# First-layer expert pieces as one 512-wide product into two banks, with the halves added on ScalarE and VectorE

## The reference

```python
def one_chunk(xc):
    ...
    sc, ci = lax.top_k(cand, PEER_TOPK)
    e = jnp.take_along_axis(i1, ci // PEER_TOPK, axis=-1) * PEER_NKEYS \
        + jnp.take_along_axis(i2, ci % PEER_TOPK, axis=-1)
    g = jax.nn.softmax(sc, axis=-1)
    u_sel = u[e]
    v_sel = v[e]
    pre = jnp.einsum("td,thkd->thk", xc, u_sel).astype(f32)
    act = (jax.nn.gelu(pre, approximate=False) * g).astype(v.dtype)
    return jnp.einsum("thk,thkd->td", act, v_sel)
```

## Time and profile before

| | |
|---|---|
| Median of 3 runs | 3540.41 us (3538.41 to 3542.09) |
| Profiled execution: its own time | 3537.68 us |
| Profiled execution: span, first to last instruction | 3535.9 us |
| TensorE matmuls busy | 3373.6 us (95%) |
| TensorE weight loads busy | 2988.4 us (85%) |
| VectorE busy | 2445.0 us (69%) |
| ScalarE busy | 1535.7 us (43%) |
| Mean granted TensorE clock | 0.982 of full |
| TensorE's share of the chain that ended last | 79% |

### The profile page before, as it was taken

The page is one execution under the profiler, slowest core; times in us unless marked ns, Lnnn a source line. Parts: engine busy times, 40 slices in busy tenths (PEclk is TensorE's granted clock), DMA queues, the critical chain, the costliest instruction groups (busy, mean ns, idle before and its releaser), DMA issues.

```text
span 3535.9 us, 54258 instructions
## 1 busy us (share of the span) xinstructions
PE 3373.6 (95%) x20894; PEld 2988.4 (85%) x20894; DVE 2445.0 (69%) x4176; ACT 1535.7 (43%) x1752; POOL 229.4 (6%) x48
## 2 busy tenths in 40 slices
PE   6899999999999999999999999999999999899998
PEld 1889999888888889899998878888878788888787
DVE  6667997777886759995557767556557575555474
ACT  1544454343333534453333335454455454544553
POOL 0005700000000028200000000000000000000000
PEclk9999999999999999999999999999999999999999
DMA  8434467778885234566666765533435455333353
GB/s 360 179 108 158 162 223 253 264 273 281 288 284 180 107 137 177 190 226 229 210 212 234 243 226 203 202 144 120 157 143 191 174 184 198 136 139 145 144 189 133
DMA packets 165987, 689.96 MB, mean 195 GB/s; under 512 B 11701, under 2 KB 78029, under 8 KB 92249
## 3 DMA queue, kind: packets, MB, share of 16 engines
q1 hardware_dynamic: 161432, 663.84, 52.1%
q10 hardware_dynamic: 4290, 22.54, 1.8%
HBM read 650.66 MB, written 35.68 MB: 194 GB/s over the span
## 4 chain that ended last, share of the span: by engine, by line
PE 79%; DVE 12%; ACT 3%; issue 2%; DVEq 1%; DMA 1%; PEld 1%; ACTq 0%; PEldq 0%
PE ps L1074 20%; PE ps L769 16%; PE ps L804 9%; PE ps L775 8%; PE ps L832 8%; PE ps L810 5%; PE ps L1052 3%; PE ps L839 3%; PE ps L860 2%; ACT weights_upper L1321 1%; DVE weights_lower L1744 1%; DMA work<-in_mem 1%; DVE position_hot L2073 1%; PE ps L866 1%; DVE position_hot L2076 1%
## 5 line engine op out<-in xcount | busy, mean ns | idle before, releaser
L1321 ACT ACTIVATE weights_upper<-weights 128x2048 fp32r<-128x2048 f32 x520 | 996.0, 1917 | 1603.2 <-PE ps L769 567.6
L1744 DVE TENSOR_TENSOR weights_lower<-weights,weights_upper 128x2048 fp32r<-128x2048 f32 x476 | 1089.8, 2290 | 643.9 <-ACT weights_upper L1321 643.6
L769 PE MATMUL ps<-hT_lower,weights_upper 128*128 128x256 f32 x2560 | 367.3, 286 | 2.8 <-DVE hT_lower L1757 2.6
L769 PE MATMUL ps<-hT_upper,weights_upper 128*128 128x256 f32 x2560 | 364.1, 285 | 0.0
L769 PEld LDWEIGHTS ps<-hT_lower,weights_upper 128*128 128x128 f32 x2560 | 334.2, 193 | 8.9 <-DVE hT_lower L1757 3.7
L775 PE MATMUL ps<-hT_upper,weights_lower 128*128 128x256 f32 x2560 | 333.6, 283 | 4.1 <-POOL weights_lower L697 4.1
L769 PEld LDWEIGHTS ps<-hT_upper,weights_upper 128*128 128x128 f32 x2560 | 334.7, 194 | 0.0
L775 PEld LDWEIGHTS ps<-hT_upper,weights_lower 128*128 128x128 f32 x2560 | 318.7, 192 | 4.9 <-POOL weights_lower L697 4.9
L804 PE MATMUL ps<-hT_span,weights_upper 128*128 128x512 f32 x1344 | 320.6, 391 | 0.0
L697 POOL TENSOR_TENSOR weights_lower<-weights,weights_upper 128x2048 fp32r<-128x2048 f32 x44 | 229.2, 5223 | 1202.8 <-ACT weights_upper L1321 1202.8
L804 PEld LDWEIGHTS ps<-hT_span,weights_upper 128*128 128x128 f32 x1344 | 247.0, 188 | 47.8
(11 more groups left out here) (375 smaller groups left out, 4202.3 us busy)
## 6 DMA issues: line engine op xcount, KB each, us to landing
weights<-in_parts SPq DMA_DIRECT2D x264, 1024.0 KB, 4.8
weights<-in_experts SPq DMA_DIRECT2D x256, 1024.0 KB, 4.9
scr<-gates SPq DMA_DIRECT2D x32, 1024.0 KB, 8.5
weights<-in_ada_w SPq DMA_DIRECT2D x12, 2048.0 KB, 13.1
work<-in_ada_s SPq DMA_DIRECT2D x96, 256.0 KB, 5.3
gates<-h SPq DMA_DIRECT2D x16, 1024.0 KB, 4.8
gates<-work SPq DMA_DIRECT2D x16, 1024.0 KB, 4.8
mod<-in_row ACTq DMA_DIRECT2D x3, 1536.0 KB, 6.3
```

The costliest lines, as they stand in the source:

```text
L769: m = mm(bank[:, e * T:(e + 1) * T], up[:, c, e * P:(e + 1) * P], s_[:, c, :], start=(e == 0 and n == 0 and c == 0), stop=False, skip_grou ...
L1321: f(upper[:, p_.r % SPLIT, :], raw[:, p_.r, :], ACT.Copy).then_inc(upper_ready, 1)
L1744: v.tensor_tensor(lower[:, s, :], raw[:, p_.r, :], upper[:, s, :].bitcast(F32), ALU.subtract)\
```

## The change

In the interleaved stretch of both layers (first-layer pieces with t at least `AHEAD`, 24 in each layer) `doubled` replaces `by_feature`: one matmul, 512 wide, multiplies a block of upper weights with the lower and the upper part of the input at once. The two parts of the result stand side by side in a bank, so a piece fills two banks, one for each block of 128 experts, and the two halves of each must be added. ScalarE copies the first halves into `gact`, VectorE adds the second halves to them (`halves_added`) and frees the banks, and ScalarE applies Gelu in place one step later (`gelu_of_sum`). The banks are laid out anew: U in 0 and 2, the second banks in 1 (`Ux0`) and 3 (`Ux1`), G in 6 and 7 ahead of acc, the row in 3 in turn with `Ux1`.

```diff
@@ -152,11 +152,17 @@
...
     p.fill("eT", 2, bank=4)
+    p.fill("G", 2, bank=6, times=GROUPS)
     p.fill("acc", 4, bank=4)
-    p.fill("U", 2, bank=0, times=TURNS, parts=1)
-    p.fill("G", 2, bank=2, times=GROUPS)
-    if not before:
-        p.fill("row", 1, bank=2, times=ADA_TILES)
+    p.fill("U", 1, bank=0, times=TURNS, parts=1)
+    p.fill("U", 1, bank=1, times=TURNS, parts=1, start=1)
+    p.fill("Ux0", 1, bank=1, times=TURNS - AHEAD, parts=1)
+    for n, (layer, t, u) in enumerate(expert_order()):
+        if layer == 0 and u == 1 and t >= AHEAD:
+            p.fill("Ux1", 1, bank=3 - t, parts=1, start=t)
+        for tile in range(0 if before else ADA_TILES):
+            if ada_sub_step(KC * tile + KC - 1) + 2 == n:
+                p.fill("row", 1, bank=3 - tile, start=tile)
...
@@ -507,8 +513,11 @@
...
-        hT_up = parts_at("hT_upper", [P, KC, T], hT_at)
-        hT1 = hT_up, parts_at("hT1_lower", [P, KC, T], mod_at)
+        step = (hT_at - mod_at) // (4 * T)
+        hT1_span = parts_at("hT1_span", [P, step + KC, T], mod_at)
+        hT_up = hT1_span[:, step:step + KC, :]
+        hT1 = hT_up, hT1_span[:, 0:KC, :]
+        hT1_both = [hT1_span[:, c:c + step + 1:step, :] for c in range(KC)]
...
@@ -780,6 +789,23 @@
...
+            def doubled(p_, banks, src, both):
+
+
+                up, lo = halves_of(p_, KC)
+                pe.wait_ge(*p_.upper())
+                for e in range(2):
+                    for c in range(KC):
+                        m = mm(banks[e].rearrange("p (n t) -> p n t", n=2), up[:, c, e * P:(e + 1) * P], both[c],
+                               start=(c == 0), stop=False, skip_group_check=True)
+                m.then_inc(upper_used, 1)
+                pe.wait_ge(*p_.lower())
+                for e in range(2):
+                    for c in range(KC):
+                        m = mm(banks[e][:, T:2 * T], lo[:, c, e * P:(e + 1) * P], src[0][:, c, :],
+                               start=False, stop=(c == KC - 1), skip_group_check=True)
+                m.then_inc(parts_done, 1)
...
@@ -1020,16 +1046,21 @@
                 def first_layer(n, t, u):
 
                     pe.wait_ge(*k.free("U", u, t))
-                    by_feature(expert_part(l, 0, n), k.bank("U", u), hT1)
+                    if t < AHEAD:
+                        by_feature(expert_part(l, 0, n), k.bank("U", u), hT1)
+                    else:
+                        second = ("Ux1", t) if u else ("Ux0", 0, t - AHEAD)
+                        pe.wait_ge(*k.free(*second))
+                        doubled(expert_part(l, 0, n), (k.bank("U", u), k.bank(*second[:2])), hT1, hT1_both)
...
                     for tile in range(ADA_TILES if l + 1 < DEPTH else 0):
                         if ada_sub_step(KC * tile + KC - 1) + 2 == n:
-                            pe.wait_ge(*k.free("row", 0, tile))
+                            pe.wait_ge(*k.free("row", tile))
                             pe.wait_ge(S("ada_used"), KC * tile + KC)
-                            mm(k.bank("row")[0:1, :], ones[:, 0:1], ada_acc[tile % 2], start=True, stop=True,
-                               skip_group_check=True).then_inc(k.fill_sem("row"), 1)
+                            mm(k.bank("row", tile)[0:1, :], ones[:, 0:1], ada_acc[tile % 2], start=True, stop=True,
+                               skip_group_check=True).then_inc(k.fill_sem("row", tile), 1)
...
@@ -1459,7 +1490,20 @@
                     act.wait_ge(*expert_part(l, 0, n).done())
                     if t >= AHEAD:
                         act.wait_ge(S("gated"), l * (2 * TURNS) + (2 * (t - AHEAD) + 2))
-                    f(gact[t % AHEAD][:, u, :, :], k.bank("U", u), ACT.Gelu).then_inc(k.empty_sem("U", u), 1)
+                    mine = gact[t % AHEAD][:, u, :, :]
+                    if t < AHEAD:
+                        f(mine, k.bank("U", u), ACT.Gelu).then_inc(k.empty_sem("U", u), 1)
+                        return
+                    banks = k.bank("U", u), k.bank(*(("Ux1", t) if u else ("Ux0", 0)))
+                    for e in range(2):
+                        m = f(mine[:, e, :], banks[e][:, 0:T], ACT.Copy)
+                    m.then_inc(S("hidden_first"), 1)
+
+                def gelu_of_sum(t, u):
+
+                    act.wait_ge(S("hidden_sum"), l * 2 * (TURNS - AHEAD) + 2 * (t - AHEAD) + u + 1)
+                    mine = gact[t % AHEAD][:, u, :, :]
+                    f(mine, mine, ACT.Gelu).then_inc(S("gelu"), 1)
...
                 def ada_take(tile):
 
-                    act.wait_ge(*k.filled("row", 0, tile))
...
@@ -1498,6 +1542,8 @@
...
+                    if n > 2 * AHEAD and expert_order()[n - 1][0] == 0:
+                        gelu_of_sum(*expert_order()[n - 1][1:])
                     if layer == 0:
                         gelu(n, t, u)
...
@@ -2102,7 +2148,10 @@
...
-                    v.wait_ge(*k.emptied("U", u, t))
+                    if t < AHEAD:
+                        v.wait_ge(*k.emptied("U", u, t))
+                    else:
+                        v.wait_ge(S("gelu"), l * 2 * (TURNS - AHEAD) + 2 * (t - AHEAD) + u + 1)
...
@@ -2130,6 +2179,17 @@
...
+                def halves_added(t, u):
+
+                    v.wait_ge(S("hidden_first"), l * 2 * (TURNS - AHEAD) + 2 * (t - AHEAD) + u + 1)
+                    mine = gact[t % AHEAD][:, u, :, :]
+                    second = ("Ux1", t) if u else ("Ux0", 0)
+                    v.tensor_tensor(mine[:, 0, :], k.bank("U", u)[:, T:2 * T], mine[:, 0, :], ALU.add)\
+                        .then_inc(k.empty_sem("U", u), 1)
+                    v.tensor_tensor(mine[:, 1, :], k.bank(*second)[:, T:2 * T], mine[:, 1, :], ALU.add)\
+                        .then_inc(k.empty_sem(*second), 1)
+                    v.drain().then_inc(S("hidden_sum"), 1)
...
@@ -2144,6 +2204,8 @@
                         lower_part(expert_part(l, 0, n + SPLIT))
                     elif l + 1 < DEPTH:
                         lower_part(part(firsts[l + 1], 0, "xbc", n + SPLIT - EXPERTS))
+                    if layer == 0 and t >= AHEAD:
+                        halves_added(t, u)
```

9 lines of the change are left out of this document (5 added, 4 removed).

## The result

| | before | after |
|---|---|---|
| Median of 13 runs each | 3540.99 us (3538.41 to 3549.91) | 3548.66 us (3543.99 to 3550.93) |
| Profiled execution: its own time | 3537.68 us | 3548.97 us |
| Span | 3535.9 us | 3547.2 us |
| Mean granted TensorE clock | 0.982 | 0.975 |

A forecast was written before the change was run, and what follows sets the result against it. TensorE was taken to bound the interleaved stretches. Wide products saving 9.2 us against new waits of 6.6 and 2.7 gave +0.1 us, so a median of 3540.5 us, range 3533.5 to 3547.0.

The forecast's parts named there:

- The gain: First-layer pieces of both interleaved stretches: a wide matmul replaces two, saving 0.19 us a piece, 9.2 us over 48.
- the slack of VectorE and ScalarE: Interleaved stretches: added copies and additions hide behind TensorE's 5.57 us piece; VectorE's fullest layer 0 step keeps 0.9 us.
- the five places: Layer 0: row products of tiles 2 and 5, and later bank 3 uses at tiles 1, 4 and 7, forecast to wait.
- New wait 1: Layer 0, tiles 2 and 5: row products wait for bank 3, just filled by the preceding piece; 3.3 us each, 6.6 total.
- New wait 2: Layer 0, tiles 1, 4, 7: pieces wait for bank 3 until ScalarE takes the row; 0.9 us each, 2.7 total.
- rival B: TensorE's clock falls to half after the two long row-product waits in layer 0: +4.4 us, 3544.9 us; chance 14%.
- The sum: Whole kernel: -9.2 + 6.6 + 2.7 = +0.1 us, so a median of 3540.5 us.
- Theory 2: Formed after the result: the new layout or wide products cost something by themselves, outside the interleaved stretch too.
- A: Layer 0: waits on bank 3 mostly absent; 3533.9 us, or 3531.2 without any new wait; chance 12%.
- C: Interleaved stretches: the wide product saves nothing because its halves are read 40 KB apart; +9.3 us, 3549.8 us; chance 6%.
- D: Layer 0: VectorE falls behind, each of 24 steps 0.4 us late; +9.6 us, 3550.1 us; chance 6%.

The follow-up runs named there:

- Layer 1 alone: The change switched off in layer 0 and kept in layer 1, against the kernel before: 3538.14 us, ratio 0.9990.
- The shift by six products: Six products of zeros added behind piece 87 of layer 0 in the kernel before, nothing else changed: 3551.11 us, ratio 1.0031 against that kernel.

## Why the prediction was wrong

- **The gain** was right: 0.19 us a piece. Layer 1 alone and layer 1 of the changed kernel show 4.8 us by the landmarks, for 4.6 forecast, and the slack of VectorE and ScalarE held. Neither engine made TensorE's matmuls wait outside the five places.
- **New wait 1** was right in place, number and chain: 3.1 us of idle time, a start 3.2 late by the page's own times, for 3.3 forecast. The run with the additions first shows that the subtraction ahead of them was 1.1 us of it, and that ScalarE's copies come next in the chain. **New wait 2** was right: 0.9 us, three times.
- **The step that failed** is the one on the clock. I put the clock behind the two new waits at nothing, since the idle stretches of 3.2 us are "shorter than the one that left the clock alone", and gave 14% to rival B. Two rows of one trace, 3.52 us without and 4.34 us with a fall, are no bound between them. The clock fell behind both waits of 3.13 us, for 4.2 us; the same 3.52 us were followed by a fall in other executions, and in the run with the additions first 2.0 us were. The trace of the kernel before could have said so: it has falls behind an idle stretch of 3.57 us at 2308 and behind shorter ones, of 2.39 us at 95, 2.55 at 102 and 3.06 at 2822. The last of these, with its windows:

```profile
2821.81 5.44 PE L741 MATMUL ps<-diag,x_res 128*128 128x128 f32 x32 [3.06 <-DVE diag L2208]
```

```profile
2822.00:2824.00 2.00, 2.00 (x16) 2.00 (x15) 2.00 (x2) 0.00 (x0) 0.00 (x0) 0.77 0.25 78
2824.00:2826.00 2.00, 2.00 (x11) 2.00 (x11) 0.33 (x1) 0.60 (x2) 0.00 (x0) 0.50 0.17 57
```

- **Rival B** came true, and its price for layer 0 was right in sum, 4.4 us for 4.2 measured, but by luck in part: it was put at 2.2 us for each wait, and the two cost 2.8 and 1.4. The warning for B from the Trainium skill, "TensorE: Matmul & The Clock Gate", section "Why this matters for your kernels", that idle gaps between bursts of matmuls bring the lower clock back, holds here: the two gaps of 3.13 us did. My remark that the trace agreed with it for the longer gap only was wrong, by the shorter ones just listed.
- **The sum** was local: local terms, and everything after them unchanged. With B it gives 3544.9, and 3.8 us were still missing by the medians; by the interval of the ratio it is between 0.2 and 5.2 us. By the landmarks they lie where no instruction changed, +1.1 between the layers and +5.9 in the second block, of which some 3 us are the luck of the profiled execution of before, which lay 2.7 to 3.3 us under its median. The shift by six products shows that such an amount can come from a shift alone: 5.2 us of work, nearly the changed kernel's 5.4 us at the head of the second block, make the whole 10 to 11 us slower. That it was the shift in the changed kernel too is likely and not shown. Theory 2 is not needed: with six products of zeros in the wait the second block of a changed kernel took 1439.9 us, 2.0 over before, with the same layout and the same wide products. That they cost 1 or 2 us by themselves is not excluded.
- **Open**: what sets the clock's falls, and so which shift is a good one. Idle time is not all of it: in the trace before, the clock stood at half from 2444.2 to 2457.9, where TensorE had been multiplying 15 and 64 columns at a time, and its longest idle gap was 0.35 us (see the window below). The time of the second block in single profiles runs from 1437.9 to 1448.4 us over the kernels here, and I can't say ahead of a run what a given shift will give.

```profile
2446.00:2448.00 2.00, 2.00 (x12) 2.00 (x11) 1.00 (x4) 0.00 (x0) 0.00 (x0) 0.50 0.01 4
```

- **Rivals**: A did not occur, since the row products did wait; C did not, at 0.229 us a wide matmul; D did not, since no piece waited for the lower weights.

The version that the experiments point to, wide products in both layers and the row products moved, is 0.21% faster than before (0.12 to 0.29) and 14 us faster than the changed kernel, of which 13.5 are layer 0's stretch (512.6 against 499.1): 9.1 us of waits and 4.2 us of low clock.

## What to carry to other kernels

When a change takes a second buffer out of a shared pool, look for the odd user of that buffer: here a product that runs eight times in the interleaved stretch, at places that a table of steps sets, cost more than the 24 pieces around it gained in that layer. Price an idle stretch of TensorE with the clock behind it, and when a trace shows one idle stretch that kept the clock, take it as one draw and not as a limit; if the wait can't be moved, fill it, but not beyond its end. To price it, look up every fall of the clock in the trace and the idle stretch ahead of each, and not two stretches alone. A difference of 0.1 or 0.2% in a kernel with many such stretches may be the shift and not the change: pad the old kernel by the same amount and compare, over many executions, since the one that is profiled can be the slowest or the fastest of them.

## What the runs showed of the hardware

- The same idle stretch of TensorE, 3.52 us at one place of the second block, left the clock at full in 4 of 13 traces and was followed by half the clock in 9. An idle stretch of 2.0 us was followed by it at tile 2 and not at tile 5 of one trace (additions first). The idle stretches of 0.7 us, where the piece is 0.9 us late, never were.
- The clock also stood at half for 13.7 us with TensorE busy: in the trace before from 2444.2, at first with matmuls of 64 columns, with no idle gap over 0.35 us.
- Three products of zeros in a wait of 3.2 us kept the clock at 1.00 and shortened layer 0's stretch by 4.3 us (508.3 against 512.6); six, 2 us too long each time, won 0.4 (512.2).
- Adding 5.2 us of TensorE work in one place made the program about 11 us slower, and 1.7 us of work 5 to 8, the latter hardly clear of its work.
- A wide matmul with a moving operand from two places 40 KB apart takes 0.229 us, as one from two other places, and one of zeros in plain float32, 512 wide, 0.87 us.
